# The opening of a two-block transformer kernel: modulation, pooling and first norm placed between the filter units

## The reference

```python
mod_x = silu(c) @ mod_w + mod_b                 # 1024 x 6144
sh1, sc1, g1, sh2, sc2, g2 = split(mod_x, 6)
hx = x * (1.0 + sc1) + sh1
outs = [centred_window_mean(hx_g, w) - hx_g for g, w in enumerate((2, 4, 8, 16))]
ox = (einsum('blgc,gcd->blgd', stack(outs), pool_w)) * pool_scale
x = layer_norm(ALPHA * x + g1 * ox, ln_g[0], ln_b[0])
x = layer_norm(ALPHA * x + g2 * swiglu(x * (1.0 + sc2) + sh2, ffn_w_in, ffn_w_out), ...)
# hyena_filters: three 64-wide sine layers, then 64 x 4096, times decay(t), then a real transform
```

## Time and profile before

| what | us |
|---|---|
| median of three runs | 2053.82 |
| range of the three | 2051.52 to 2066.12 |
| the profiled execution | 2051.8 |
| its span from the first to the last instruction | 2050.5 |

### The profile page before, as it was taken

How to read it: one execution, slowest core, us unless ns; L and a number is a source line. 1 busy time by engine, 2 the same in 40 slices (tenths; PEclk the granted TensorE clock), 3 DMA queues, 4 the chain that set the end, 5 groups by cost and what they waited for, 6 DMA issues and landing times.

```text
span 2050.5 us, 19838 instructions
## 1 busy us (share of the span) xinstructions
PE 1828.0 (89%) x7906; PEld 1457.1 (71%) x7906; DVE 1030.2 (50%) x1484; ACT 619.4 (30%) x866; POOL 755.6 (37%) x348
## 2 busy tenths in 40 slices
PE   3882799999999899989999998999566989999997
PEld 1552688888877666768888886787565768888886
DVE  6998633332134758364444224423999454444224
ACT  1222322222224444243333213322222243333222
POOL 3123234444432311324444443343444324444442
PEclk9886799999998999989999998999878989999998
DMA  5671122322222110112232222432111312322222
GB/s 214 263 291 54 39 93 93 102 93 101 95 83 68 62 33 30 62 57 97 94 102 93 94 99 76 154 95 80 62 42 41 113 62 93 101 95 96 97 95 73
DMA packets 48149, 193.99 MB, mean 95 GB/s; under 512 B 5655, under 2 KB 5975, under 8 KB 43384
## 3 DMA queue, kind: packets, MB, share of 16 engines
q1 hardware_dynamic: 47480, 188.52, 27.1%
q10 hardware_dynamic: 576, 4.19, 0.5%
HBM read 180.11 MB, written 12.58 MB: 94 GB/s over the span
## 4 chain that ended last, share of the span: by engine, by line
PE 74%; DVE 19%; ACT 3%; POOL 2%; issue 1%; DMA 1%; ACTq 0%; SPq 0%; DVEq 0%
PE ps L414 24%; PE ps L416 23%; PE ps L415 23%; DVE mod_sums L1356 2%; POOL w_lo L1166 2%; PE ps L525 1%; DVE x_residual L1759 1%; DVE n_values L1488 1%; DVE filter_taps L1339 1%; DVE act_lo L1493 1%; PE ps L741 1%; DVE x_residual L1749 1%; ACT w_hi L865 1%; DVE x_residual L1751 1%; DVE hy_product_lo L1763 1%
## 5 line engine op out<-in xcount | busy, mean ns | idle before, releaser
L1166 POOL TENSOR_TENSOR w_lo<-w_raw,w_hi 128x1024 fp32r<-128x1024 f32 x258 | 622.9, 2415 | 984.0 <-ACT w_hi L865 984.0
L414 PE MATMUL ps<-act_hi,w_hi 128*128 128x512 f32 x1428 | 573.7, 402 | 75.4 <-POOL act_lo L1224 36.6
L415 PE MATMUL ps<-act_lo,w_hi 128*128 128x512 f32 x1428 | 566.3, 397 | 0.0
L416 PE MATMUL ps<-act_hi,w_lo 128*128 128x512 f32 x1428 | 565.7, 396 | 0.0
L865 ACT ACTIVATE w_hi<-w_raw 128x1024 fp32r<-128x1024 f32 x258 | 273.4, 1060 | 744.4 <-PE ps L416 736.9
L414 PEld LDWEIGHTS ps<-act_hi,w_hi 128*128 128x128 f32 x1428 | 274.5, 192 | 149.9 <-issue 51.8
L416 PEld LDWEIGHTS ps<-act_hi,w_lo 128*128 128x128 f32 x1428 | 274.5, 192 | 58.7
L415 PEld LDWEIGHTS ps<-act_lo,w_hi 128*128 128x128 f32 x1428 | 275.1, 193 | 56.6 <-issue 1.0
L414 PE MATMUL ps<-f_hidden_hi,w_hi 128*128 128x512 f32 x528 | 209.0, 396 | 1.9 <-POOL w_lo L1166 1.9
L416 PE MATMUL ps<-f_hidden_hi,w_lo 128*128 128x512 f32 x528 | 207.6, 393 | 0.0
L415 PE MATMUL ps<-f_hidden_lo,w_hi 128*128 128x512 f32 x528 | 206.0, 390 | 0.0
(11 more groups left out here) (266 smaller groups left out, 2298.4 us busy)
## 6 DMA issues: line engine op xcount, KB each, us to landing
w_raw<-in_w_stream SPq DMA_DIRECT2D x258, 512.0 KB, 3.3
mod_ring<-in_mod_w SPq DMA_DIRECT2D x16, 1536.0 KB, 10.4
hy_filter<-spectra SPq DMA_DIRECT2D x8, 1024.0 KB, 4.7
spectra<-filter_spectra SPq DMA_DIRECT2D x4, 1024.0 KB, 9.7
spectra<-filter_spectra ACTq DMA_DIRECT2D x4, 1024.0 KB, 7.3
decay<-in_decay SPq DMA_DIRECT2D x1, 2048.0 KB, 13.7
x_residual<-in_xT SPq DMA_DIRECT2D x8, 256.0 KB, 10.8
x_spill<-x_residual SPq DMA_DIRECT2D x8, 256.0 KB, 9.9
```

Source lines behind the costliest of these rows:

```text
L414: PE.matmul(o, lh, rh, start=start, stop=False, **kw)
L415: PE.matmul(o, lh, rl, start=False, stop=False, **kw)
L416: return PE.matmul(o, ll, rh, start=False, stop=stop, **kw)
L1166: GP.tensor_tensor(B.WL[:, c % 2, :], B.WR[:, c % 2, :], f32(B.WH[:, c % 2, :]), ALU.subtract).then_inc(S.w_lo, 1)
```

## The change

The three parts `filters`, `pooling` and `first_norm` become one function `start` on each engine, and `affine` is spread over it.

The modulation weights come as 48 tiles of 512 KB (one for each 128 outputs) in a ring of three. Tile t goes to TensorE if t is a multiple of 4 (eight one-column matmuls), otherwise the vector engine multiplies it by a row that holds silu(c) and sums along the row in the same instruction. Ten tiles are worked off between the sine layers, the rest in batches after `MOD_BATCHES`: two tiles of a batch before the unit's butterflies, the others behind them. The sums are read at four points (`mod_read`).

The windows of pooling become matmuls of the untransposed `x` with a band matrix of 144 columns (`pool_windows`, 32 matmuls), so that the vector engine has one subtraction for each tile. Pooling and norm stand in the units: pooling input on ScalarE after unit 0, windows after unit 1, the two weight chunks after units 2 and 3, mean after 4, squares after 5, inverse rows after 6, the scaled values around unit 7. All four low halves of a unit are on GpSimd. The loads of `x`, the tables and the first half of the decay move to ScalarE's queue; each unit's spectra are written by SP right after its butterflies, and the second half of the decay table is fetched after unit 2. The four tap tiles use three banks (`TAP_BANKS`). The order of the units becomes half, order, kind.

The core of the diff:

```diff
+        self.hx, self.hidn = self.val, self.x_sum
+        sb = Place(nc, stage_at)
+        self.MW = sb("mod_ring", [P, MOD_RING, D])
...
-MC = 3
-N_TRANSFERS = 16
+MOD_ORDER = (1, 0, 2, 3, 4, 5)
+MOD_RING = 3
+MOD_BATCHES = (10, 16, 22, 28, 34, 40, 45, 48, 48)
+MOD_READS = (16, 24, 40, 48)
+MOD_COLUMN = 16
+BAND = P + 2 * PAD
+BAND_AT = (0, P - PAD, 2 * P - PAD, T - BAND)
+BAND_KIND = (0, 1, 1, 2)
+TAP_BANKS = (0, 1, 2, 0)
 
 
...
+    def mod_tile(t):
+        PE.wait_ge(S.mod_in[t % MOD_RING], 16 * (t // MOD_RING + 1))
+        for n, first in enumerate(MOD_READS[:-1]):
+            if t == first:
+                PE.wait_ge(S.mod_read, n + 1)
+        at = MOD_COLUMN + t // 4
+        for k in range(KD):
+            ins = PE.matmul(ps[:, 7, at:at + 1], B.MW[:, t % MOD_RING, k * P:(k + 1) * P], B.sc[:, k:k + 1],
+                            start=(k == 0), stop=(k == KD - 1))
+        ins.then_inc(S.mod_pe, 1)
+    def mod_tiles(low, high):
...
+    def tap(v, q):
+        n, order, kind = unit_parts(v)
+        if q == 3:
+            PE.wait_ge(S.decayed, 4 * v + 1)
+        elif v:
+            PE.wait_ge(S.decayed, 4 * v - (0, 2, 1)[q])
+        PE.matmul(ps[:, TAP_BANKS[q], :], B.hidn[:, q * P:(q + 1) * P], B.fsd[:, kind, order, n * 512:(n + 1) * 512],
...
+    def pool_windows():
+        PE.wait_ge(S.x_tok_in, 16)
+        PE.wait_ge(S.band_in, 16)
+        for k in range(KD):
+            if k == 1:
+                PE.wait_ge(S.odd_copied, 4)
+            if k >= 2:
+                PE.wait_ge(S.diff, k - 1)
+            for s in range(4):
+                ins = PE.matmul(ps[:, POOL_BANKS[k], BAND_AT[s]:BAND_AT[s] + BAND], B.x_tok[:, s, k * P:(k + 1) * P],
+                                B.band[:, 4 * BAND_KIND[s] + k // 2, :], start=(s == 0), stop=(s == 3),
+                                skip_group_check=True)
+            ins.then_inc(S.pooled, 1)
...
+    def pool_linear(cc, v):
+        wh, wl = chunk(cc)
+        for m in range(4):
+            tile = 4 * cc + m
+            if m < 2:
+                PE.wait_ge(S.diff, 8)
+                PE.wait_ge(S.odd_copied, 2 * v + 2)
+                if cc:
+                    PE.wait_ge(S.x_ready, 3 + m)
+            else:
+                PE.wait_ge(S.x_ready, tile - 1)
+            for k in range(2):
+                a = 2 * (m // 2) + k
+                PE.wait_ge(S.diff_lo, 4 * cc + a + 1)
+                ins = mm3(ps[:, POOL_BANKS[tile], :], wh[:, 2 * m + k, :], wl[:, 2 * m + k, :], AH[:, a, :], AL[:, a, :],
+                          k == 0, k == 1)
+            if m == 3:
+                ins.then_inc(S.w_used, 1)
+            else:
+                ins.then_inc(S.pool_done, 1)
...
+    def first_norm_squares(v):
+        PE.wait_ge(S.odd_copied, 2 * v + 2)
+        for k in range(KD):
+            PE.wait_ge(S.ln_square, k + 1)
+            square = B.sq[:, k, :] if k < 4 else B.val[:, k, :]
+            for q in range(4):
+                ins = PE.matmul(ps[:, 5, q:q + 1], square[:, q * P:(q + 1) * P], B.mean_w[:, 0:1],
+                                start=(k == 0 and q == 0), stop=False, skip_group_check=True)
+        ins.then_inc(S.ln_turned, 1)
...
+        PE.wait_ge(S.fw_sums, 4)
+        for q in range(4):
+            tap(0, q)
+                for q in range(3):
+                    tap(v + 1, q)
+            for group in range(4):
+                if group == 0:
+                    if v == 2:
+                        PE.wait_ge(S.diff, 8)
+                    elif v in (3, 4):
+                        PE.wait_ge(S.x_ready, 4 * v - 8)
+                    elif v == 6:
+                        PE.wait_ge(S.ln_stat, 1)
+                transform(v, group)
+            if v < 7:
+                tap(v + 1, 3)
+                mod_tiles(MOD_BATCHES[v], MOD_BATCHES[v + 1])
+            if v == 1:
+                pool_windows()
+            elif v in (2, 3):
+                pool_linear(v - 2, v)
+            elif v == 4:
+                first_norm_mean()
+            elif v == 5:
+                first_norm_squares(v)
+            elif v == 6:
+                inverse_rows_of(0, 3)
...
+        SC.dma_start(B.fwo, B.a["hy_fw_out"]).then_inc(S.fw_out_in, 16)
+        SC.dma_start(B.tabr, B.a["dft_fwd"]).then_inc(S.dft_in, 16)
+        SC.dma_start(B.decay[:, :, :], B.a["decay"][0]).then_inc(S.decay_in[0], 16)
+        SC.dma_start(B.x_tok[:, :, :], B.a["x_tokens"]).then_inc(S.x_tok_in, 16)
+        SC.dma_start(B.band[:, :, :], B.a["pool_band"]).then_inc(S.band_in, 16)
+        for k in range(KD):
+            SC.dma_start(X[:, k, :], B.a["xT"][k * P:(k + 1) * P, :]).then_inc(S.x_in, 16)
...
+                    SC.wait_ge(S.spectrum, 4 * v - (1 if q < 2 else 0))
...
+        def pool_parts(cc):
+            for a in range(4):
+                k = 4 * cc + a
+                if cc == 0:
+                    SC.wait_ge(S.diff, k + 1)
+                    SC.activation(B.hx[:, k, :], B.hx[:, k, :], ACT.Identity,
+                                  bias=B.MOD[:, k:k + 1]).then_inc(S.diff_whole, 1)
+                else:
+                    SC.wait_ge(S.w_used, 1)
+                SC.wait_ge(S.diff_whole, k + 1)
+                SC.activation(AH[:, a, :], B.hx[:, k, :], ACT.Copy).then_inc(S.diff_hi, 1)
+        for v in range(8):
+            filter_hi(v)
+            odd_part(v, 0)
+            odd_part(v, 1)
+            if v == 0:
+                w_hi(0)
+                w_hi(1)
+                SC.wait_ge(S.x_in, 16 * KD)
+                SC.wait_ge(S.affine, 1)
+                SC.wait_ge(S.fw_sums, 4)
+                for k in range(KD):
+                    SC.activation(B.hx[:, k, :], X[:, k, :], ACT.Identity, bias=B.MOD[:, k:k + 1],
+                                  scale=B.AFF[:, 0, 0, k:k + 1]).then_inc(S.pool_in, 1)
+            elif v == 1:
+                pool_parts(0)
+                for k in range(4, KD):
+                    SC.wait_ge(S.diff, k + 1)
+                    SC.activation(B.hx[:, k, :], B.hx[:, k, :], ACT.Identity,
+                                  bias=B.MOD[:, k:k + 1]).then_inc(S.diff_whole, 1)
+            elif v == 2:
+                for k in range(KD):
+                    SC.activation(X[:, k, :], X[:, k, :], ACT.Copy, scale=ALPHA_1).then_inc(S.x_scaled, 1)
+                pool_parts(1)
+            elif v == 4:
+                w_hi(2)
+                w_hi(3)
+            elif v == 5:
+                for k in range(KD):
+                    SC.wait_ge(S.ln_centred, k + 1)
+                    SC.activation(B.sq[:, k, :] if k < 4 else B.val[:, k, :], X[:, k, :],
+                                  ACT.Square).then_inc(S.ln_square, 1)
...
+        for v in range(8):
+            if v == 6:
+                norm(0)
+            filter_lo(v)
+            if v == 0:
+                w_lo(0)
+                w_lo(1)
+            elif v in (1, 2):
+                pool_lo(v - 1)
+            elif v == 4:
+                w_lo(2)
+                w_lo(3)
...
+            VE.tensor_tensor_reduce(out=src, in0=src, in1=B.c_row[:, :], scale=1.0, scalar=0.0, op0=ALU.mult,
+                                    op1=ALU.add, accum_out=B.MOD[:, m:m + 1]).then_inc(S.mod_dve, 1)
...
+            mod_tiles((0, 4, 7)[layer], (4, 7, 10)[layer])
...
+        for q in range(4):
+            decayed(0, q)
+        for v in range(7):
+            low, high = MOD_BATCHES[v], MOD_BATCHES[v + 1]
+            for q in range(3):
+                decayed(v + 1, q)
+            mod_tiles(low, low + 2)
+            butterfly(v)
+            decayed(v + 1, 3)
+            mod_tiles(low + 2, high)
+            if v == 1:
+                for k in range(KD):
+                    VE.wait_ge(S.pooled, k + 1)
+                    VE.wait_ge(S.pool_in, k + 1)
+                    VE.scalar_tensor_tensor(out=B.hx[:, k, :], in0=ps[:, POOL_BANKS[k], :],
+                                            scalar=AFF[:, 0, 0, k:k + 1], in1=B.hx[:, k, :], op0=ALU.mult,
+                                            op1=ALU.subtract).then_inc(S.diff, 1)
+            elif v in (2, 3):
+                cc = v - 2
+                for m in range(4 * cc, 4 * cc + 4):
+                    if m % 4 == 3:
+                        VE.wait_ge(S.w_used, cc + 1)
+                    else:
+                        VE.wait_ge(S.pool_done, 3 * cc + m % 4 + 1)
+                    VE.wait_ge(S.x_scaled, m + 1)
+                    VE.scalar_tensor_tensor(out=X[:, m, :], in0=ps[:, POOL_BANKS[m], :], scalar=AFF[:, 0, 1, m:m + 1],
+                                            in1=X[:, m, :], op0=ALU.mult, op1=ALU.add).then_inc(S.x_ready, 1)
+            elif v == 4:
+                VE.wait_ge(S.ln_mean, 1)
+                for k in range(KD):
+                    VE.tensor_tensor(X[:, k, :], X[:, k, :], ps[:, 3, :], ALU.subtract).then_inc(S.ln_centred, 1)
+            elif v == 5:
+                VE.wait_ge(S.ln_turned, 1)
```

(31 more changed lines are left out.)

519 lines of the change are left out of this document (184 added, 335 removed).

## The result

The changed kernel takes 2110.19 us (median of four runs, 2104.87 to 2117.18). Over the same four rounds the kernel before takes 2059.57 (2051.52 to 2066.12). The ratio is 1.026, with a 95% interval of 1.0224 to 1.0296: slower by 2.6%. The forecast was 2080 with a range up to 2104. The sign was the likeliest one on record; the size was too small, and the result lies outside the range.

The account below looks back on a forecast made before the run. It took the vector engine as the bound from 42 to 160 us, then a serial chain: terms sum to 271.5 us against 243.9, so 2051.8 + 27.6 = 2079.4, said as 2080; own range 2062 to 2100, 8 in 10 2024 to 2104.

Parts of the forecast that it names:

- The sign: Whole kernel: slower was given 0.50, same 0.33, faster 0.17.
- Units 1 and 3: Opening: from the end of the previous unit's butterflies to their own, 29.0 and 35.3 us.
- the band matmuls: Unit 2's pooling windows on TensorE: 32 matmuls cost 8.3 to 16.6 us, taken as 10.5.
- the values: After unit 7, the norm's scaled values up to the last low half of the first norm: 13.3 us.
- Both halves of the chain: Opening: serial halves, transforms and butterflies, 12.7 us a unit, plus waits for tiles that SP issues behind spectrum writes.
- The start: Up to the end of unit 0's butterflies: 55 us, first decay product kept at 41.6, difference bounded by -3 and +8.
- B(0): End of unit 0's butterflies, forecast at 55 us; the number in brackets is the unit.
- Landings: After a unit's butterflies: a batch's fifth tile lands at about 5 us, 8.4 if its first is TensorE's; chunk 2 at 4.5.
- The clock: TensorE after a pause: 12 matmuls at 0.427 us instead of 0.228, 2.4 us each time the transforms follow one.
- the two traces run alike: From the third up-projection chunk on, the kernels before and after were to show no further difference.
- The first two: Ring keeps ahead: without clock prices opening 218.6 us, total 2026, chance 0.17; with them 244.5, 2052, chance 0.29.
- The third: Low halves alternate with row sums, GpSimd losing about 3 us in seven units, 21 in all: 2101 us; chance 0.12.

Follow-up runs that it names:

- e5_petile: Changed kernel, each batch's fifth tile issued before the spectrum writes and TensorE's first tile of a batch (units 1, 3, 5) done before the transforms; 2084.65 us (1.0124).
- e10_first: Changed kernel, ScalarE and GpSimd making the next unit's halves first in units 1 to 3 and 6, chunks 2 and 3 split later; 2073.1 us (1.0101).
- e14_start3: e11_all with xT issued behind the twelfth tile and the untransposed x and band table before unit 0's spectrum writes, all on SP; 2051.25 us (0.9971).
- e13_ring4: e11_all with a fourth slot in the tile ring and the whole batch issued before the unit's spectrum writes; 2042.56 us (0.9913).
- run 7: Not a follow-up run: in "run 7 to 10 matmuls at the low clock" the word is a verb, said of the transforms.
- e11_all: Changed kernel with e5_petile and e10_first joined, the second decay table and chunks 2 and 3 moved, and a 704-byte pad; 2054.82 us (0.9982).
- e15_filler: e13_ring4 with 112 filler matmuls that nobody reads in five pauses of TensorE; 2032.13 us (0.9879).

## Why the prediction was too low

**What held.** The bound moved off the vector engine, and the opening became a chain: low halves, tile landings, clock. Units 1 and 3, the band matmuls (10.5 us forecast, 10.46 measured) and the values came out within a microsecond. The row sum took 1.21 us where I took 1.2. Both halves of the chain that I described are real: undoing one (e5_petile) or the other (e10_first) gives 30 us each, and both give 52.6, more than the excess of 47.4.

So the path was right and terms of the sum were too small. The sum of 2079.4 lacks 19.8 us in the opening and 5.7 in the hidden values' pace; another 5.7 are not the change's, since the median of the kernel before is 2059.57 in these rounds and I counted from 2053.82. That makes some 2110.6, and 2110.19 was measured. The pieces below are read from the trace; of them only the start's transfers and the pace were switched by a run.

**The start** is the step that failed most: "I let the first decay product stay at 41.6 ... I bound the difference by -3 and +8." The term of 55 us measured 64.1. The product came at 48.68, near the edge of my own bound, and B(0) 2.0 later still, as the taps did not run ahead. I had kept the start because its chain of sines is unchanged. But ten tiles now go through a ring of three while everything else is loaded beside them (the transfer engines 0.90 busy at 329 GB/s in the first 42 us): TensorE waits for tile 0 until 22.2. What I should have summed is the bytes: 329 GB/s over 42 us are 13.8 MB, of which the tables and x are 9.2 and the tiles the rest. e14_start3 gives 5 of the 7 us back by moving 5.1 MB behind, and a ring of four gives 2 without that (e13_ring4).

**Landings**, sized for an unloaded moment: TensorE got tile 20 at B(1) + 10.3 where I had 8.4, and tile 32 at B(3) + 10.2; chunk 2 landed at B(4) + 6.0 instead of 4.5. The queue in front was two spectrum writes and SP's own wait, as said, but these three came 1.5 to 1.9 us later than that, 5.2 in all. Tile 20 was issued 1.9 us after B(1) where I had 0.9, and took 8.4 us to land where I had 7.5. Tile 44 landed as forecast (B(5) + 8.0).

**The clock**, 2.4 us "each time that the transforms follow a pause": right for units 1, 2, 3 and 5, whose transforms follow pauses of 3.4 to 15.3 us and run 7 to 10 matmuls at the low clock. Unit 6 did not pay it: TensorE came from its own work there, and all but the third and fourth steps are at the high pace. I left it out of unit 7, whose transforms follow a pause of 4.32 us and start slow (granted 0.59 from 270 to 274; 13.6 us where I had 11.4), of the squares (13.9 us measured, all at the low clock, 11.1 forecast) and of TensorE's tiles (3.58, where I took 2.1 of a range of 2.1 to 3.5).

**The hidden values' pace**, 5.7 us over the whole run, stood in no term. I wrote that behind the third up chunk "the two traces run alike"; they don't, and a pad that moves the buffers switches it.

**The rivals.** The first two needed a ring that keeps ahead; the runs show what that takes: e13_ring4, in which no tile is waited for in the units, has 224.3, between my 218.6 (no clock prices) and 244.5 (with them), but it needed the order of the halves too. The third, row sums beside low halves, is real and smaller than its 21 us here: GpSimd loses 3 us in low halves and 2 in weight halves, and 11 of 36 sums are stretched, by 11 us in all, of which 7.6 in the units. The Trainium skill's rule ("SBUF — State Buffer", section "Who interferes with whom") is borne out: a sum of two SBUF inputs beside a low half takes 2.3 us, its own 1.2 and nearly one low half of 1.25. It weighs more the better the rest gets. The row that I gave for it, 5.74 us of L1308, is of an instruction with one input, which takes 0.42 us at 7.26 in the same trace: a wait beside GpSimd too, but not of the kind of a row sum.

The chances were off as well: faster 0.17 and same 0.33 leaned on the ring keeping ahead, and SP's order, which I had read correctly, speaks against that.

What stays open: whether the start can be as short as before at all. Each place tried for the tables delayed something else, and fewer tiles ahead of unit 0 were not tried. Nor was it tried to leave two low halves of a unit on the vector engine, as before; that too would shorten the serial chain, and what the move of them to GpSimd costs by itself is not shown.

## What to carry to other kernels

When a chain of waits takes the place of a busy engine, look at each in-order queue for what stands behind a wait without needing it: moving one transfer ahead of two writes and one piece of TensorE's work ahead of a wait gave 30 us here without one operation less, letting the next unit's splits go first gave 30 too, and both gave 53. A change that relieves the bound engine needs this ordering before it pays: the same design lost 2.6% in one order, comes level in another (e11_all), and wins 1.2% with a fourth slot and fillers on top (e15_filler). And sum the bytes of a start against what the transfers reach, whatever the chain of operations there says.

## What was not expected of the hardware

- The pace of these float32 matmuls goes with where the buffers lie that hold their moving operand: 0.2326 us with them 704 bytes lower, 0.229 at the old place, switched both ways. Other buffers moved along, so that it is the moving operand's address is argued, not shown, and which property of the address decides was not tried.
- The size of a late transfer matters less than its turn: tiles of 1/64 of the size still made TensorE wait 5.3 of 9.8 us and gave 13.5 us; full tiles in another turn gave 30.2.
- Two vector sums of 1.2 us took 7.78 and 5.50 beside GpSimd's sums and a low half of 128x2048: several times the shorter operation, not twice.
- One-column matmuls did not raise the clock: 32 products for the squares kept TensorE busy for all of 238.8 to 252.5 us at a granted clock of 0.50.
- Filler matmuls in pauses of 3.5 to 4.8 us raised the granted clock of 25 us from 0.86 to 1.00, and the opening ended 4.8 us earlier.
